# Score passes of a differential attention: row-tiled f32 against stacked f32r

## The reference

```python
def diff_attention(q, k, v, lam, rel_table):      # 4 heads, each with two maps m of 64 features
    def block(i):                                 # 128 queries
        s = jnp.einsum('bqhmd,bkhmd->bhmqk', qb, kf) * scale
        ...
        s = jnp.where(rel >= 0, s + bias[None, :, None], NEG)
        pm = jax.nn.softmax(s, axis=-1)
        w = pm[:, :, 0] - lam * pm[:, :, 1]
        return jnp.einsum('bhqk,bkhe->bqhe', w.astype(v.dtype), v)
```

## Time and profile before

| | |
|---|---|
| median of 3 runs | 2490.55 us (2488.79 to 2491.5) |
| span of the profiled execution | 2486.4 us |
| around that span, against the median | 4.15 us |
| PE, DVE, ACT busy | 99%, 60%, 45% of the span |
| granted clock of TensorE | 1.00 in both stretches of the change |

### The profile page before, as it was taken

One profiled execution on the slowest core, in us unless ns is written; L12 is line 12 of the kernel. 1 busy time (PEld: TensorE's weight loads), 2 busy tenths in 40 slices (PEclk: granted clock), 3 DMA queues, 4 the chain that ended last, 5 costly groups with the idle time before them and its releaser, 6 DMA issues.

```text
span 2486.4 us, 32337 instructions
## 1 busy us (share of the span) xinstructions
PE 2467.6 (99%) x11940; PEld 1961.0 (79%) x11940; DVE 1486.3 (60%) x2518; ACT 1125.7 (45%) x2012; POOL 25.9 (1%) x18
## 2 busy tenths in 40 slices
PE   9999999999999999999999999999999999999999
PEld 7887888888776788888887777778877777777887
DVE  7987656566769753433456655664465665466435
ACT  6675433433546543442445543442354554444234
POOL 0000000000000000000000000000020000000002
PEclk9999999999999999999999999999999999999999
DMA  7633466666221123222221211222223121122233
GB/s 305 217 105 134 167 203 206 206 204 205 85 85 69 64 89 103 101 95 95 101 102 69 77 63 70 77 81 93 102 85 110 62 75 68 64 83 77 93 109 111
DMA packets 77902, 280.34 MB, mean 113 GB/s; under 512 B 8640, under 2 KB 8896, under 8 KB 77504
## 3 DMA queue, kind: packets, MB, share of 16 engines
q1 hardware_dynamic: 61056, 219.60, 25.1%
q10 hardware_dynamic: 16704, 58.79, 7.1%
HBM read 276.26 MB, written 2.10 MB: 112 GB/s over the span
## 4 chain that ended last, share of the span: by engine, by line
PE 92%; DVE 4%; ACT 2%; DMA 1%; issue 0%; SPq 0%; ACTq 0%
PE ps L222 26%; PE ps L224 25%; PE ps L223 25%; PE ps L1817 2%; PE ps L1914 2%; DVE wl L217 1%; PE ps L1887 1%; PE ps L1719 1%; PE ps L1157 1%; PE ps L1821 1%; PE ps L1219 1%; ACT wh L214 1%; PE ps L1776 1%; PE ps L1194 1%; PE ps L408 1%; PE ps L1992 1%
## 5 line engine op out<-in xcount | busy, mean ns | idle before, releaser
L217 DVE TENSOR_TENSOR wl<-raw,wh 128x1024 fp32r<-128x1024 f32 x372 | 456.7, 1228 | 592.0 <-ACT wh L214 592.0
L222 PE MATMUL ps<-xh,wl 128*128 128x512 f32 x1744 | 696.1, 399 | 3.8 <-DVE wl L217 2.4
L224 PE MATMUL ps<-xh,wh 128*128 128x512 f32 x1744 | 680.3, 390 | 0.0
L223 PE MATMUL ps<-xl,wh 128*128 128x512 f32 x1744 | 679.7, 390 | 0.0
L214 ACT ACTIVATE wh<-raw 128x1024 fp32r<-128x1024 f32 x372 | 392.8, 1056 | 600.7 <-PE ps L224 589.7
L222 PE MATMUL ps<-bh,wl 128*128 128x512 f32 x1174 | 463.3, 395 | 2.7 <-DVE crow L1181 1.5
L224 PE MATMUL ps<-bh,wh 128*128 128x512 f32 x1174 | 457.3, 390 | 0.0
L223 PE MATMUL ps<-bl,wh 128*128 128x512 f32 x1174 | 457.2, 389 | 0.0
L222 PEld LDWEIGHTS ps<-xh,wl 128*128 128x128 f32 x1744 | 327.1, 188 | 122.4 <-issue 37.6
L224 PEld LDWEIGHTS ps<-xh,wh 128*128 128x128 f32 x1744 | 327.3, 188 | 69.9
L223 PEld LDWEIGHTS ps<-xl,wh 128*128 128x128 f32 x1744 | 327.6, 188 | 65.5 <-issue 1.2
(11 more groups left out here) (322 smaller groups left out, 2543.4 us busy)
## 6 DMA issues: line engine op xcount, KB each, us to landing
raw<-in_w SPq DMA_DIRECT2D x388, 512.0 KB, 3.2
bA<-in_ada ACTq DMA_DIRECT2D x74, 512.0 KB, 4.5
bC<-in_ada SPq DMA_DIRECT2D x9, 512.0 KB, 12.0
bD<-in_ada ACTq DMA_DIRECT2D x8, 512.0 KB, 4.6
bS<-in_attn_bias ACTq DMA_DIRECT2D x8, 512.0 KB, 3.2
bD<-in_ada SPq DMA_DIRECT2D x7, 512.0 KB, 14.3
bC<-in_ada ACTq DMA_DIRECT2D x6, 512.0 KB, 4.3
h<-in_x SPq DMA_DIRECT2D x4, 512.0 KB, 7.7
```

The source lines that it names most:

```text
L217: e.tensor_tensor(wl[p][:], raw[p][:], wh[p][:].bitcast(F32), ALU.subtract)\
L222: e.matmul(out, wl[p][:, blk, 0:M], xhi, start=start, stop=False)
L223: e.matmul(out, wh[p][:, blk, 0:M], xlo, start=False, stop=False)
L224: return e.matmul(out, wh[p][:, blk, 0:M], xhi, start=False, stop=stop)
```

## The change

The two scores matmuls of a step are no longer f32 with 64 contraction rows, one for each half of the array. For each map the query tile is now 128 rows, all f32r: the rounded query in one half, the rest (query less rounded query) in the other. The key is held twice over 128 rows: rounded key in both halves (`kh`, in `bh`), and the rest in both halves (`kl`, in `bl`). Each map is two f32r passes on the whole array, by `kh` and by `kl`, into one PSUM bank.

A query unit's output was one copy on ACT. It is now two copies of 64 partitions on ACT, with rounding, and two subtractions on DVE that read PSUM and write the other half of the partitions. A key unit's output was one copy on ACT. It is now two rounding copies on ACT and two subtractions on DVE; then, behind the weight work of `split`, two copies from SBUF to SBUF on ACT and two on DVE that fill the other halves. PE waits for the last of these before a head's first scores (`key_ready`). The bank of a query or key unit comes free with DVE's last subtraction, and no longer with ACT's copy.

```diff
--- before.py
+++ after.py
@@ -1621,6 +1621,11 @@
                 bank, used = it.at[m]
                 e.wait_ge(s_bank[bank], used + 2)
 
+            def key_ready(it):
+
+                need(it.name + "hh1")
+                need(it.name + "ll1")
+
             def sum_out(it, m):
 
                 bank, used = it.at[m]
@@ -1654,6 +1659,27 @@
                     e.activation(it.dst, src, ACT.Copy).then_inc(s_bank[bank], 1)
                 if it.kind == "gate" and act:
                     e.activation(it.dst, src, ACT.Tanh, scale=0.5).then_inc(s_bank[bank], 1)
+                lower, upper = slice(0, HD), slice(HD, P)
+                if it.kind == "query":
+                    q0, q1 = it.dst
+                    if act:
+                        e.activation(q0[lower, :], src[lower, :], ACT.Copy)
+                        done(e.activation(q1[upper, :], src[upper, :], ACT.Copy), it.name + "hi")
+                    if dve:
+                        need(it.name + "hi")
+                        e.tensor_tensor(q0[upper, :], src[lower, :], q0[lower, :].bitcast(F32), ALU.subtract)
+                        e.tensor_tensor(q1[lower, :], src[upper, :], q1[upper, :].bitcast(F32), ALU.subtract)\
+                         .then_inc(s_bank[bank], 1)
+                if it.kind == "key":
+                    (kh0, kh1), (kl0, kl1) = it.dst
+                    if act:
+                        done(e.activation(kh0[lower, :], src[lower, :], ACT.Copy), it.name + "hi0")
+                        done(e.activation(kh1[upper, :], src[upper, :], ACT.Copy), it.name + "hi1")
+                    if dve:
+                        need(it.name + "hi1")
+                        done(e.tensor_tensor(kl0[lower, :], src[lower, :], kh0[lower, :].bitcast(F32), ALU.subtract), it.name + "lo0")
+                        e.tensor_tensor(kl1[upper, :], src[upper, :], kh1[upper, :].bitcast(F32), ALU.subtract)\
+                         .then_inc(s_bank[bank], 1)
                 if it.kind == "silu":
                     if act:
                         done(e.activation(bD[:, 10, :], src, ACT.Tanh, scale=0.5), it.name + "th")
@@ -1670,6 +1696,17 @@
                                                ALU.mult, ALU.subtract).then_inc(s_bank[bank], 1)
                 if act or not low_later:
                     split(it.u + 2, 0, 0)
+                if it.kind == "key":
+                    if act:
+                        need(it.name + "hi0")
+                        done(e.activation(kh0[upper, :], kh0[lower, :].bitcast(F32), ACT.Copy), it.name + "hh0")
+                        need(it.name + "hi1")
+                        done(e.activation(kh1[lower, :], kh1[upper, :].bitcast(F32), ACT.Copy), it.name + "hh1")
+                    if dve:
+                        need(it.name + "lo0")
+                        done(e.tensor_copy(kl0[upper, :], kl0[lower, :].bitcast(F32)), it.name + "ll0")
+                        e.wait_ge(s_bank[bank], used + 2)
+                        done(e.tensor_copy(kl1[lower, :], kl1[upper, :].bitcast(F32)), it.name + "ll1")
                 for m in range(sums_first, 2) if it.kind == "sum" else ():
                     sum_out(it, m)
                 for m in range(2) if it.last else ():
@@ -1715,9 +1752,9 @@
                         for m in range(2):
                             if n:
                                 need(f"{s}{n - 1}st{m}")
-                            r = slice(HD * m, HD * m + HD)
-                            done(e.matmul(ps[2 + m][:, 0:nk(n)], q(n // NT)[r, P * i:P * i + P], k(n // NT)[r, 0:nk(n)],
-                                          start=True, stop=True), f"{s}{n}sc{m}")
+                            x, (kh, kl) = q(n // NT)[m][:, P * i:P * i + P], k(n // NT)
+                            e.matmul(ps[2 + m][:, 0:nk(n)], x, kh[m][:, 0:nk(n)], start=True, stop=False)
+                            done(e.matmul(ps[2 + m][:, 0:nk(n)], x, kl[m][:, 0:nk(n)], start=False, stop=True), f"{s}{n}sc{m}")
 
                 def maximum(n):
                     if dve:
@@ -2055,7 +2092,12 @@
                         done(e.activation(bT[:, t, :], ps[2 + t][:], ACT.Copy, scale=sm[:, t:t + 1]), f"{n}v{t}")
 
 
-                dq, dk = (lambda t: bC[:, t % 2, :]), (lambda t: bC[:, 2 + t % 2, :])
+                def dq(t):
+                    return [bh[:, 4 * (t % 2) + m, :] for m in range(2)]
+
+                def dk(t):
+                    return [[x[:, 4 * (t % 2) + 2 + m, :] for m in range(2)] for x in (bh, bl)]
+
                 da_rows = lambda t: bD[:, 6 + t, :].rearrange("p (i f) -> p i f", i=NT)
                 s = n + "D"
                 scores, maximum, exponentials, combine, turn, turned, values, results = da_pair(
@@ -2065,7 +2107,7 @@
 
                 def scored(t):
                     return (lambda: need(f"{s}{4 * t - 5}sc1")) if t > 1 else None
-                heads = [[Unit("copy", f"{n}aq{t}", dq(t), scored(t), ready=n + "n" if t == 0 else None), Unit("copy", f"{n}ak{t}", dk(t), scored(t))] for t in range(4)]
+                heads = [[Unit("query", f"{n}aq{t}", dq(t), scored(t), ready=n + "n" if t == 0 else None), Unit("key", f"{n}ak{t}", dk(t), scored(t))] for t in range(4)]
                 silu = [Unit("silu", f"{n}az{t}", bS[:, t, :]) for t in range(4)]
                 banks(NARROW)
                 for it in heads[0] + silu[:1]:
@@ -2116,6 +2158,7 @@
                         if pe and (k + 1) % NT == 0:
                             for it in heads[(k + 1) // NT]:
                                 out_of(it)
+                            key_ready(heads[(k + 1) // NT][1])
                         scores(k + 1)
                         maximum(k + 1)
                     outs = fill(halves, plan[k + 1], state)
```

## The result

| | before | after |
|---|---|---|
| median, runs side by side | 2491.5 us (2488.79 to 2495.57) | 2505.37 us (2503.97 to 2506.86) |
| span of the profiled execution | 2486.4 us | 2503.6 us |
| predicted | | 2494.2 us, range 2484 to 2503 |

The account below looks back on a forecast made before the run. PE, busy 99% of the span, was taken as the bound: 8.6 us saved and 12.2 us of stalls give +3.6 on 2486.4, 2490.0; with 4.15 us around the span 2494.2 us, range 2484 to 2503.

Parts of the forecast that it names:

- What PE saves: Score passes on PE: eight sets go from 30.1 to 21.5 us, saving 8.6 us.
- the 3.3 us of old waits: PE's existing waits for DVE at scores with 512 keys, 0.92 and twice 0.36 us per layer, would go.
- The stall behind a key unit: PE's transposes wait for w behind six key units, 2.2 or 1.76 us each; all stalls net +12.2 us.
- start-to-start price of the new instructions: New ACT and DVE output work: 0.49 us per ACT copy, 0.61 per DVE subtraction, 0.35 per DVE copy.
- 0.4 and 0.6 us: Lateness of ACT at the key's first copy, from the query unit's work: 0.4 in the first group, 0.6 in others.
- the 0.5 for the last group: Small PE waits at the last group, 0.5 us within the 15.5 us of stalls.
- Granted clock 1.00: PE's granted clock in the stretch would still be 1.00, which is 2.4 GHz.
- DVE's queue ahead of w decides: Rival: DVE copies cost 0.61 us each, or lateness and hand-overs are larger; 2497.3 to 2499 us, chance 0.27.
- Narrow passes are dear: Rival: all f32r score passes cost 0.227 us, or more below 512 columns; 2497 to 2503 us, chance 0.09.
- the saving stands alone: Rival: w reaches PE's transposes in time, so the saving of 9.7 us stays; 2481 to 2485 us, chance 0.09.
- Late copies of ACT: ACT's two late key copies delay the copy of transposed w by 1 us, costing nothing.
- The first head's key copies: Covered by a silu unit of 5.4 us on PE, costing nothing; without cover up to 2 us a layer.

Follow-up runs that it names:

- e1: Changed kernel with one rounding copy per query and key unit, low parts and stacking left out, f32r passes kept: 2482.4 us, ratio 0.9961 to before.
- e5: Changed kernel plus 16, 10 and 10 unused passes on old data right ahead of each layer's three waiting transposes: 2502.7 us, ratio 1.0044 to before.
- e4: Changed kernel with the new ACT and DVE instructions on 128 partitions instead of 64, same number and order, stacking left out: 2496.07 us, ratio 1.0017.
- e13: Changed kernel with all new ACT and DVE instructions on partitions 0 to 63, upper halves left out: 2497.28 us, ratio 1.0023 to before.
- e9: Changed kernel with the query's output as one rounding copy on ACT for both maps, its rest left out: 2501.78 us, ratio 1.0045 to before.
- e6: Changed kernel with both of DVE's low copies of each key unit moved to GpSimd: 2499.39 us, ratio 1.0032 to before.
- e11: Changed kernel with DVE's weight work later, both key low copies on GpSimd and plan 1, 1, 2, 2; nothing left out: 2481.87 us, ratio 0.9966.
- e12: Kernel before the change with DVE's weight work later and plan 1, 1, 2, 2: 2489.43 us, ratio 0.9992 to before.
- e2: Kernel with the f32 scores of before beside all the changed kernel's new ACT and DVE work, its output unread: 2516.56 us, ratio 1.0097 to before.
- e10: Changed kernel with DVE's weight work issued behind the next iteration's combination and maxima, nothing removed: 2491.24 us, ratio 1.0003 to before.
- e8: Changed kernel with both key low copies on GpSimd plus 9 and 8 passes on old data ahead of the waiting transposes: 2496.99 us, ratio 1.0024.

## Why the prediction was wrong

The first layer's stretch, from the last pass of L1992 (L2029 after) to the first of L2191 (L2234), cut at PE's transposes. "Behind a key unit" is the iteration whose transposes wait.

| us | before | e1 | e5 | after |
|---|---|---|---|---|
| up to the first group's transposes of 128 keys | 29.40 | 28.85 | 28.84 | 28.85 |
| behind a key unit, three | 3.91, 4.78, 4.79 | 3.91, 4.45, 4.45 | 7.05, 7.37, 7.38 | 7.05, 6.31, 7.38 |
| the next (512 keys), three | 5.44, 4.83, 4.82 | 4.83, 4.57, 4.57 | 4.95, 4.84, 4.83 | 6.93, 4.83, 5.99 |
| rest of the group, two | 14.36, 14.35 | 13.88, 13.90 | 13.91, 13.88 | 13.74, 13.90 |
| last group and tail | 41.07 | 39.95 | 41.58 | 41.25 |
| sum | 127.75 | 123.36 | 134.63 | 136.23 |

Both layers: 255.4 before, 270.95 after, +15.55 us, against +3.6 forecast. The missing 11.95 us by steps, each a difference between the four columns, so that they close by construction. Outside the stretches the two profiles differ by 1.65 us more; the change's has low clock there (at 25 to 45 and 735 us) and that of before has none.

**What PE saves: right.** The four kinds of step became shorter by 0.05, 0.43, 0.33 and 0.35 us for 128 to 512 keys (e1 against before, read between transposes where PE does not wait), 1.16 together and 9.3 us in eight sets; forecast were 8.6 (the sum with the floor is 9.9, not 9.7). Narrow f32r passes, on which a rival rested, are 0.12 us apart at 256 columns:

```profile
1324.00 0.28 PE L1757 MATMUL ps<-bl,bh 128*128 128x256 f32 x1
1324.12 0.28 PE L1756 MATMUL ps<-bh 128*128 128x256 f32 x1
1324.24 0.28 PE L1757 MATMUL ps<-bl,bh 128*128 128x256 f32 x1
```

But the 3.3 us of old waits, which I also took off, did not go with it. Behind the key units the steps with 512 keys are 0.61, 0.26 and 0.26 us shorter in e1, where the passes alone save 0.35: of the 0.92 and twice 0.36 that I counted as waits, 0.26 went at the first and nothing at the others. e1's stretches are 4.39 us shorter each at full clock, 8.8 in both, where saving and waits together were put at 11.9. **Miss: 3.1 us.**

**The stall behind a key unit: right in place, too small, by the start-to-start price of the new instructions.** That price is the step that failed: 0.49 us for ACT's copy, 0.61 for a subtraction and 0.35 for a copy on DVE, taken over from instructions that start on the same partition as their neighbours (the 0.49 is in the earlier trace rows, not 6). That 64 partitions take as long as 128 was right. But the new instructions alternate between rows 0 to 63 and 64 to 127, none overlaps the one ahead, and each costs 0.10 us more. It counts twice.

In the key unit's own row, from ACT's first copy to the end of w are 3.90 us before and 6.02 after (1330.07 to 1336.09), +2.12, where 0.79 + 0.70 = 1.49 stood. Without the alternation the same piece is 5.31 us (e4) and 5.30 us (e13): +1.4, what was reckoned. Six key units at 0.64: **3.8 us.** The Trainium skill, VectorE: DVE Perf Modes, section Two Vector instructions with no wait between them, states this for DVE: an instruction whose input or output starts in another group of 32 partitions than the last one's is held until all earlier ones have finished. The rows of the change and of e13 agree with it, and the rule was there to be read before the prediction.

In the query unit's row it makes the key's first copy late. I took 0.4 and 0.6 us. With the clock up it is 1.00 at T1 (copy at 1303.33, pass start 1301.89, 0.44 between them before) and 1.07 at T2 (e5: 1328.68, 1327.17). e9 takes the query's work away and T1's wait falls by 0.99. The copy and the pass of the change, and then of e13:

```profile
1301.89 0.40 PE L224 MATMUL ps<-xh,wh 128*128 128x512 f32 x1
1303.33 0.59 ACT L1676 ACTIVATE bh<-ps 64x512 fp32r<-64x512 f32 x1
```
```profile
1301.81 0.40 PE L224 MATMUL ps<-xh,wh 128*128 128x512 f32 x1
1302.65 0.58 ACT L1676 ACTIVATE bh<-ps 64x512 fp32r<-64x512 f32 x1
```

With all of them at partition 0 the lateness is 0.40 at T1 in both layers, and 0.55 and 0.60 at T2 and T3 of the second layer, where the clock stayed up: the figures of the forecast (the 0.6 was a choice between 0 and 0.8, so its closeness is partly luck). So its account of ACT's idle time and of PE's lead held, and what lies above it is the same 0.10 us again: from the query's first copy to the key's first are 6.96 us in the change and 6.35 in e13 at T1, while PE takes 5.5 in both to its last pass. Two at 0.6, four at 0.47: **3.1 us.**

Against this the scores with 512 keys come only 1.4 us later in all six places (e5 against e1) and not 3.6, which with the 0.5 for the last group gives back 2.7. As a whole, e5 less e1 is 19.35 us in both layers at full clock, against 15.5: **miss 3.85 us**; the parts give 4.2. With even starting partitions the whole would have been below the forecast: e13 in the second layer is 5.7 us longer than e1 up to the transposes of the next-to-last step, 11.5 for two layers. The alternation costs the other 8, and e13 is 8.1 us below the change in the medians.

**Granted clock 1.00: wrong.** Two prices. In e5 the clock is 1.00 at the waits, but falls in the tail of each stretch, behind a run of narrow passes (transposes, sums and values), as it does in the change (1400 to 1404):

```profile
1396.98:1399.00 2.02, 2.02 (x16) 1.84 (x16) 1.23 (x1) 2.00 (x6) 0.00 (x0) 0.89 0.00 0
1399.00:1401.00 2.00, 2.00 (x9) 1.48 (x8) 0.89 (x4) 1.26 (x5) 0.00 (x0) 0.50 0.77 250
```

From the transposes of the next-to-last step to the end of the stretch are 12.04 and 12.03 us before, 13.67 and 13.62 in e5: **3.2 us.** That this fall is the change's doing is not shown. e1, e6, e11 and e12 have it in the second layer alone, e2 and e10 in the first alone and e4 in neither, with the same work there; in e12, which has neither the new passes nor the new work, the piece is then 13.39 us. So part of these 3.2 us may lie in the execution of before that was profiled, which had no fall at all. Of the 19 executions of before beside e5, the four with a clock of 1.0 took 2487.7 to 2488.9 us and the other fifteen 2489.95 to 2494.4. The same is in the 4.15 us that I put around the span: in the later profiles it is 1.8. The low clock behind the waits is the change less e5: 1.60 + 0.16 = **1.8 us**. In the table it takes 1.98 us from PE behind T1 (6.93 for 4.95) and gives back 1.06 at T2 (6.31 for 7.37).

3.1 + 3.85 + 3.2 + 1.8 = 11.95. I first read it otherwise: the records show PE 12 us of full speed short (6.8 and 5.1 us in the two stretches), the stretches are 15.5 us longer, and so I put some 11 us down to the clock and 4 to the forecast's mechanism. e5 and e8 took that theory away.

**Rivals.** "DVE's queue ahead of w decides" had the place and the sign, and I gave it 0.27. Its two reasons were wrong or too small: the casts are 0.42 us, not 0.68, and "a few hundredths more for each hand-over" was 0.10 for every new instruction on DVE and ACT, for a reason that I did not name. "Narrow passes are dear" is refuted, and "the saving stands alone" too. Late copies of ACT did no harm, as forecast. The first head's key copies were covered: the piece up to the first transposes is 28.85 us with or without them.

## What to carry to other kernels

Where an engine with 35% idle time stands in one row with the engine that sets the time, write its queue out from the last point at which it truly had slack; a slack counted a step later is used up by the work of the step before. Work that nobody needs soon (here the weights two units ahead) belongs behind what the bounding engine waits for: that one move was worth 14 us, the price of the whole change. And keep neighbouring instructions of DVE and ACT on the same starting partitions, or price each at its full duration.

## What the runs showed of the hardware

- The start partition: 0.71 instead of 0.61 us between subtractions of 512 columns, 0.45 instead of 0.33 between copies (DVE), 0.59 instead of 0.50 (ACT), at equal durations. e13 against the change is 8.1 us in 2500.
- Low clock behind a wait: in the two stretches of all profiled runs PE has 41 waits of 1.2 to 3.3 us. The clock fell in or behind 26 of them, the shortest 1.32 (e2), and not at 15, the longest 2.33 (e9, first layer; in the second it fell behind the same wait). In e13 it fell behind 1.95 and 1.52 in the first layer and not behind 1.98, 1.48 and 1.55 in the second. Behind those of 1.1 us and less at T1 to T3 it stayed up. So the length of the wait alone does not decide. What a fall costs is decided by who sets the pace behind it: 1.3 us in e9, but 0.75 from T1 to T2 in the change, where 26.98 us stand against 26.23 in e5.
- GpSimd's copy of 64x512 takes 0.61 us alone, but 1.67 beside DVE's weight work, which itself is not slower (1.23):

```profile
1328.97 0.61 POOL L1707 CAST bl<-bl 64x512 fp32r<-64x512 f32 x1 [22.96 <-DVE bl L1680]
1329.70 1.67 POOL L1709 CAST bl<-bl 64x512 fp32r<-64x512 f32 x1
```
```profile
1329.67 1.23 DVE L217 TENSOR_TENSOR wl<-raw,wh 128x1024 fp32r<-128x1024 f32 x1
```

  These are e6's rows. The Trainium skill, GPSIMD Engine Reference, section Specifications, says that the SBUF interfaces are shared with VectorE, with contention beside VectorE's instructions of two SBUF inputs. L217 has two, and the rows agree. In e11, where that work comes later, both copies in the loop take 0.61.
